# One root chain at each layer norm, a last norm shared with TensorE, and a third conditioning buffer for the tenth weight slot

## The chip, the cores and the metric

The kernel runs on one core of a Trainium2 chip. The metric is the device time of one execution in microseconds (us), lower is better. Before the change three executions gave 2537.12, 2537.58 and 2540.77 us, so the median is 2537.58 us.

## What is computed

Two post-norm layers over 256 tokens of width 2048, all in float32. A conditioning vector `c` gives a shift, a scale and a gate for each sub-layer.

```python
cond = jax.nn.silu(c)
for l in range(DEPTH):                                   # DEPTH = 2
    ada = (cond @ w_ada[l] + b_ada[l])[:, None, :]       # 2048 x 12288 matrix, one row of input
    sh_m, sc_m, g_m, sh_f, sc_f, g_f = jnp.split(ada, N_ADA, axis=-1)
    h = x * (1.0 + sc_m) + sh_m
    y = hybrid_mixer(h, ..., w_in[l], w_out[l], ...)     # h @ w_in (6672 columns), three head groups, @ w_out
    x = layer_norm(DEEPNORM_ALPHA * x + (1.0 + g_m) * y, ln_g[l, 0], ln_b[l, 0])
    h = x * (1.0 + sc_f) + sh_f
    y = jnp.square(jax.nn.relu(h @ w1[l])) @ w2[l]       # width 8192 between
    x = layer_norm(DEEPNORM_ALPHA * x + (1.0 + g_f) * y, ln_g[l, 1], ln_b[l, 1])
```

`layer_norm` is `(x - mean) * rsqrt(var + 1e-5) * g + b` over the 2048 columns.

## The kernel before

**Units and passes.** The tokens are two rows of 128 partitions (r = 0 and 1). Every large matrix product is cut into units: a block of 128 rows of weights by 1024 columns (512 KB). A pass is 16 units that add into four PSUM banks; there are 25 passes in a layer, 0 to 6 for `w_in`, 7 and 8 for `w_out`, 9 to 24 for the MLP in four groups, 800 units in all. To keep float32 accuracy each operand is split into a high part and a rest, and each product is three matrix products. A unit goes this way: SyncE (SP) issues its load into one of ten slots `RAW` (L477); ScalarE copies it to the high part `WH`, one of six slots (`hi_split`, L643); VectorE subtracts to get the rest `WL`, written over `RAW` (`lo_split`, L1024); TensorE multiplies (L1554 for most, L1563 for products that come out transposed, L1522 for the first pass of a sub-layer). Splits run four units ahead of TensorE (`AHEAD`). The load of a unit waits until the unit ten before it is done (`unit_done`).

**Conditioning.** `cond @ w_ada` runs beside the passes on VectorE. A block of 128 rows by 1024 columns of `w_ada` lands in one of two buffers `ADR` (L468), and one VectorE instruction multiplies it by a scalar per partition and adds it to `ACC` (`ada_mul`, L922 and L925). After 16 blocks TensorE sums `ACC` over the partitions (L1456, or L1463 for a gate). A written-out plan, `ADA_PLAN`, says beside which units the 16 blocks of each piece are added, and by which unit the sum is due. In layer 0 it puts nearly one block beside each of the first 50 units, and 16 blocks beside units 93 to 106. SP issues the load of block `a` behind the weight load that is `ADA_LAG` (6) units ahead of its place, and only when block `a - 2` has been added. SP issues in order, so a block that waits holds the weight loads behind it.

**The layer norm between sub-layers.** Of the last four units of passes 8 and 24 TensorE does one PSUM bank at a time (`last_units`, L1536), so that VectorE can begin a quarter (one row r, 512 columns) while TensorE does the next. `quarter` (L1068 to L1077) multiplies the bank by the gate, adds it to X, and takes batch statistics; after the second quarter of a row it aggregates them and prepares the variance. ScalarE takes the square root (L687), `newton` (L1044 to L1048) inverts it and improves it by one Newton step, `rstd` also makes `NMR = -mean * rstd` (L1082), and `norm` (L1087) writes the normed X. Gain and bias of the norm are folded into the next sub-layer's scale and shift. TensorE then transposes X (L1489), ScalarE applies scale and shift (`h_tiles`, L663 and L666), and the next pass starts (L1522). There are three such boundaries. All engines run program order as written; nothing is reordered.

**The last norm** (`last_layer_norm`) needs gain and bias in full: per row r and 512 columns, `centre` (L1121) is `(x - mean) * g` and `finish` (L1127) is `* rstd + b`. SP stores each of the eight pieces when it is finished (L511).

Of the kernel before, what the change touches and what calls it, by code (L numbers as in the profile page):

```python
# [17 lines left out]
P = 128  # L18
# [7 lines left out]
RAW_SLOTS, W_SLOTS = 10, 6  # L26
PRO_SLOTS = 16
AHEAD = 4
ADA_LAG = 6
# [70 lines left out]
def hybrid_trunk(nc, x, c, positions, lb_logits, w_in, w_out, w_ada, b_ada, ln_g, ln_b, hg_norm_w,  # L100
                 m_conv_w, m_conv_b, m_dt_bias, m_a_log, m_d, m_norm_w, w1, w2, consts, out):
    with ExitStack() as ctx:
# [12 lines left out]
        X = sb("X", [P, 2, D])  # L115
        HTh = sb("HTh", [P, KT, SEQ], F32R)
# [10 lines left out]
        ADR = sb("ADR", [P, 2, UW])  # L127
# [29 lines left out]
        NMR = sb("NMR", [P, 2])  # L157
        RV = sb("RV", [P, 8])
# [104 lines left out]
        ada_in = [Signal(f"ada_in{i}", 16 * 96) for i in range(2)]  # L263
# [7 lines left out]
        xT = Signal("xT", 16)  # L271
        hT_hi = Signal("hT_hi", 32)
# [6 lines left out]
        rs_in = Signal("rs_in", 7)  # L279
        rs_act = Signal("rs_act", 7)  # L280
# [134 lines left out]

        def ada_arrived(a):

            return ada_in[a % 2].sem, 16 * ((a - 64) // 2 + 1)
# [43 lines left out]
        def _(sp):  # L462
            def ada_load(a):
                q, k = divmod(a, 16)
                if a >= 64 + 2:
                    sp.wait_ge(ada_mac.sem, ada_added(a - 2))
                row, col = ADA_SEQ[q] // 12 * D + k * P, ADA_SEQ[q] % 12 * UW
                sp.dma_start(ADR[:, a % 2, :], w_ada_r[row:row + P, col:col + UW]).then_inc(ada_in[a % 2].sem, 16)  # L468

# [46 lines left out]
        def _(pool):  # L516
            link = Order(pool, order["pool"])
            pool.memset(RV[:, :], 1.0)
# [82 lines left out]
        def _(act):  # L601
# [52 lines left out]
            def h_tiles(layer, s, b):  # L654

                if b == 0:
                    act.wait_ge(cols_set.sem, cols_set.at(layer, s + 1))
                act.wait_ge(xT.sem, xT.at(layer, 8 * s + b + 1))
                for j in range(2):
                    kt = 2 * b + j  # L660
                    cols = work(s * FF0, b % 4)[:, j * SEQ:(j + 1) * SEQ]
# [22 lines left out]
            def ln_sqrt(layer, s, r):  # L684

                act.wait_ge(rs_in.sem, rs_in.at(layer, 4 + 2 * s + r))
                act.activation(RA[:, r:r + 1], RV[:, r:r + 1], ACT.Sqrt).then_inc(rs_act.sem, 1)  # L687

# [13 lines left out]
            def layer_norm(layer, s, n):  # L702

                ln_sqrt(layer, s, 0)
                for m in range(n - 2, n + 1):
                    next_split(layer, m)
                ln_sqrt(layer, s, 1)
# [203 lines left out]
        def _(dve):  # L911
# [3 lines left out]
            def ada_mul(a):  # L915

                q, k = divmod(a, 16)
                w = ADR[:, a % 2, :]
# [141 lines left out]
            def quarter(layer, s, i, p, k, passes):  # L1060
# [13 lines left out]
                if h == 1:  # L1074
                    link(ins)
                    link(dve.bn_aggr(MV[:, r, :], BN[:, r, :, :].rearrange("p a b -> p (a b)")))
                    ts(RV[:, r:r + 1], MV[:, r, 1:2], LN_EPS, None, ALU.add).then_inc(rs_in.sem, 1)  # L1077

            def rstd(layer, s, r):

                link(newton(layer, 4 + 2 * s + r, slice(r, r + 1)))
                link(stt(NMR[:, r:r + 1], MV[:, r, 0:1], -1.0, RR[:, r:r + 1], ALU.mult, ALU.mult))  # L1082
# [13 lines left out]
            def layer_norm(layer, s, p, k, passes, gate, n):  # L1096
# [18 lines left out]
            def last_layer_norm(layer, p, k, passes, gate):  # L1115

                done = {"mul": 0}

                def centre(r, ch):
                    xc, cols = X[:, r, ch * 512:(ch + 1) * 512], slice(ch * 512, (ch + 1) * 512)  # L1120
                    stt(xc, xc, MV[:, r, 0:1], LNG[:, cols], ALU.subtract, ALU.mult).then_inc(ln_mul.sem, 1)  # L1121
                    done["mul"] += 1

                def finish(r, ch, mul):
                    xc, cols = X[:, r, ch * 512:(ch + 1) * 512], slice(ch * 512, (ch + 1) * 512)
                    dve.wait_ge(ln_mul.sem, mul)
                    stt(xc, xc, RR[:, r:r + 1], LNB[:, cols], ALU.mult, ALU.add).then_inc(x_out.sem, 1)  # L1127
# [3 lines left out]
                dve.wait_ge(ln_gb_in.sem, ln_gb_in.at(layer, 64))  # L1131
                quarter(layer, 1, 0, p, k, passes)
                quarter(layer, 1, 1, p, k, passes)
                centre(0, 0)
                rstd(layer, 1, 0)
                centre(0, 1)
                quarter(layer, 1, 2, p, k, passes)
                finish(0, 0, 1)
                centre(0, 2)
                finish(0, 1, 2)  # L1140
                centre(0, 3)
                quarter(layer, 1, 3, p, k, passes)
                finish(0, 2, 3)
                finish(0, 3, 4)
                centre(1, 0)
                rstd(layer, 1, 1)
                centre(1, 1)
                finish(1, 0, 5)
                centre(1, 2)
                finish(1, 1, 6)  # L1150
                centre(1, 3)
                finish(1, 2, 7)
                finish(1, 3, 8)
# [295 lines left out]
        def _(pe):  # L1449
# [31 lines left out]
            def x_transpose(layer, s, b):  # L1481
# [3 lines left out]
                for r in range(2):  # L1485
                    pe.wait_ge(x_ready.sem, x_ready.at(layer, 6 * s + (r + 1 if b == 0 else 4 if b < 4 else 6)) - 6)
                    for j in range(2):
                        kt = 2 * b + j
                        ins = tr(work(s * FF0, b % 4)[:, j * SEQ + r * P:j * SEQ + (r + 1) * P],  # L1489
                                 X[:, r, kt * P:(kt + 1) * P], ident)  # L1490
                ins.then_inc(xT.sem, 1)
# [339 lines left out]


# [19 lines left out]
```

## Time and profile before

| what | value |
|---|---|
| median of three executions | 2537.58 us |
| the profiled execution | 2538.42 us |
| its span, first to last instruction | 2536.6 us |
| TensorE busy with matrix products | 2418.4 us, 95% of the span |
| VectorE busy | 1893.9 us, 75% |
| ScalarE busy | 1163.9 us, 46% |
| mean granted TensorE clock | 0.99 |
| HBM traffic | 249 GB/s over the span |

How to read it: TensorE is nearly always busy, so time can only be won where it waits or where it runs at the lower clock. In the timelines an instruction has its start, its duration and its shape, and in square brackets the idle time of its engine before it with what ended that. The durations overlap: an instruction of VectorE begins before the one ahead has quite ended, so the step from start to start is what counts.

### The profile page before, as it was taken

The page shows a single profiled execution, that of the slowest core. Times are in us where ns is not written, and L with a number is a line of the kernel's source. Part 1 is how long each engine was busy: PE and PEld are TensorE (multiplying, and loading weights), DVE is VectorE, ACT ScalarE, POOL GpSimd, SP SyncE. Part 2 cuts the span into 40 slices and gives each one's busy share as a digit, 9 for nine tenths or more (in the row PEclk, how much of TensorE's full clock was granted, in tenths as well). Part 3 has the DMA queues.
Part 4 walks back from the last instruction along what each step waited for, and adds up shares of the span by engine and source line. Part 5 has one row for each costly group of instructions (what it writes and reads, how often), then busy time and mean ns, then how long its engine had stood idle before and what let it go on. Part 6 is the DMA issues. An engine that isn't in the chain of part 4 may idle for free.

```text
span 2536.6 us, 36597 instructions
## 1 busy us (share of the span) xinstructions
PE 2418.4 (95%) x14933; PEld 2181.6 (86%) x14933; DVE 1893.9 (75%) x2099; ACT 1163.9 (46%) x1507; POOL 174.7 (7%) x119
## 2 busy tenths in 40 slices
PE   2599999999999999999999999999999999999997
PEld 2599987888989989989979998888898998998986
DVE  7889897878977787878777568868797555555556
ACT  0364475545533534434436446655544353443442
POOL 0002100010011011011010020001001101101001
PEclk9999999999999999999999999999999999999999
DMA  9998577887898898898865535778688656656653
GB/s 389 374 335 287 162 249 243 294 290 258 286 323 320 277 331 301 305 315 295 292 233 158 167 110 178 228 256 300 249 290 291 187 186 192 184 189 192 183 190 109
DMA packets 176396, 634.02 MB, mean 250 GB/s; under 512 B 20236, under 2 KB 20964, under 8 KB 174948
## 3 DMA queue, kind: packets, MB, share of 16 engines
q1 hardware_dynamic: 171648, 614.80, 71.7%
q0 software_dynamic: 3008, 16.32, 1.7%
q8 instruction: 118, 1.93, 0.3%
q10 hardware_dynamic: 1572, 0.56, 0.1%
q14 instruction: 50, 0.41, 0.1%
HBM read 629.50 MB, written 2.10 MB: 249 GB/s over the span
## 4 chain that ended last, share of the span: by engine, by line
PE 85%; DVE 7%; DMA 4%; issue 1%; ACT 1%; SPq 0%; DVEq 0%; ACTq 0%
PE PB L1554 42%; PE PB L1563 29%; PE PB L1522 8%; DMA ADR<-in_w_ada 2%; DMA RAW<-in_w_ada 2%; PE PB L1536 1%; DVE ACC L925 1%; DVE WL L1024 1%; DVE ACC L1015 1%; PE PB L1597 1%; PE PB L1456 1%; DVE CV L1197 1%; PE PB L1463 1%; PE PB L1489 1%; SPq L483 0%
## 5 line engine op out<-in xcount | busy, mean ns | idle before, releaser
L1024 DVE TENSOR_TENSOR WL<-RAW,WH 128x1024 fp32r<-128x1024 f32 (+1 forms) x800 | 994.2, 1250 | 481.4 <-ACT WH L643 480.6
L643 ACT ACTIVATE WH<-RAW 128x1024 fp32r<-128x1024 f32 (+1 forms) x800 | 832.3, 1044 | 1117.0 <-PE PB L1554 537.9
L1563 PE MATMUL PB<-HTh,WH 128*128 128x256 f32 x2176 | 620.9, 285 | 0.0
L1563 PE MATMUL PB<-HTh,WL 128*128 128x256 f32 x2176 | 616.9, 284 | 0.0
L1563 PE MATMUL PB<-HTl,WH 128*128 128x256 f32 x2176 | 616.8, 283 | 0.0
L925 DVE SCALAR_TENSOR_TENSOR ACC<-ADR,CT,ACC 128x1024 f32<-128x1024 f32 x300 | 393.0, 1310 | 59.8 <-DMA ADR<-in_w_ada 57.8
L1563 PEld LDWEIGHTS PB<-HTl,WH 128*128 128x128 f32 x2176 | 418.7, 192 | 0.8 <-issue 0.5
L1563 PEld LDWEIGHTS PB<-HTh,WH 128*128 128x128 f32 x2176 | 418.6, 192 | 0.8 <-issue 0.5
L1563 PEld LDWEIGHTS PB<-HTh,WL 128*128 128x128 f32 x2176 | 418.6, 192 | 0.0
L1554 PE MATMUL PB<-WH,T2h 128*128 128x512 f32 x1208 | 374.4, 391 | 0.0
L1554 PE MATMUL PB<-WL,T2h 128*128 128x512 f32 x1208 | 372.1, 389 | 0.0
L1554 PE MATMUL PB<-WH,T2l 128*128 128x512 f32 x1208 | 371.9, 389 | 0.0
L1554 PEld LDWEIGHTS PB<-WL,T2h 128*128 128x128 f32 x1208 | 226.7, 188 | 47.4
L1554 PEld LDWEIGHTS PB<-WH,T2l 128*128 128x128 f32 x1208 | 226.7, 188 | 47.3
L1554 PEld LDWEIGHTS PB<-WH,T2h 128*128 128x128 f32 x1208 | 225.8, 188 | 47.7 <-issue 1.9
L536 POOL TENSOR_TENSOR X<-X,Y 128x512 f32<-128x512 f32 x64 | 112.5, 1788 | 1356.2 <-DVE Y L1176 1356.2
L1554 PE MATMUL PB<-WH,HTh 128*128 128x512 f32 x512 | 163.9, 401 | 0.6 <-issue 0.6
L1554 PE MATMUL PB<-WL,HTh 128*128 128x512 f32 x512 | 158.8, 391 | 0.0
L1554 PE MATMUL PB<-WH,HTl 128*128 128x512 f32 x512 | 158.2, 390 | 0.0
L1554 PEld LDWEIGHTS PB<-WH,HTl 128*128 128x128 f32 x512 | 96.4, 188 | 20.9
L1554 PEld LDWEIGHTS PB<-WL,HTh 128*128 128x128 f32 x512 | 96.4, 188 | 20.8
L1554 PEld LDWEIGHTS PB<-WH,HTh 128*128 128x128 f32 x512 | 92.7, 189 | 19.1 <-issue 1.5
(288 smaller groups left out, 2124.3 us busy)
## 6 DMA issues: line engine op xcount, KB each, us to landing
RAW<-in_w SPq DMA_DIRECT2D x512, 512.0 KB, 4.6
ADR<-in_w_ada SPq DMA_DIRECT2D x320, 512.0 KB, 5.3
RAW<-in_w_in SPq DMA_DIRECT2D x192, 512.0 KB, 4.2
RAW<-in_w_ada SPq DMA_DIRECT2D x64, 512.0 KB, 15.8
RAW<-in_w_out SPq DMA_DIRECT2D x64, 512.0 KB, 5.9
RAW<-in_w_in SPq DMA_DIRECT2D x32, 264.0 KB, 2.8
GB<-in_b_ada POOLq DMA_DIRECT2D x8, 512.0 KB, 7.6
LNG<-in_ln_g POOLq DMA_DIRECT2D x4, 1024.0 KB, 7.6
```

The source lines that it names most:

```text
L536: pool.tensor_tensor(xc, xc, Y4[:, b, :], ALU.add).then_inc(x_add.sem, 1)
L643: act.activation(WH[:, wh_slot(layer, n), 0:w], RAW[:, k, 0:w], ACT.Copy).then_inc(hi_done.sem, 1)
L925: ins = stt(ACC[:, :], w, CT[:, k:k + 1], ACC[:, :], ALU.mult, ALU.add)
L1015: ins = stt(acc[:, :], block_, CT[:, k:k + 1], acc[:, :], ALU.mult, ALU.add)
L1024: tt(WL[:, k, 0:w], RAW[:, k, 0:w], WH[:, wh_slot(layer, n), 0:w].bitcast(F32), ALU.subtract).then_inc(lo_done.sem, 1)
L1197: ins = stt(dst[:, j, sh:SEQ], src[:, j, 0:SEQ - sh], cCW[:, tap, t:t + 1], dst[:, j, sh:SEQ], ALU.mult, ALU.add)
L1456: ins = mm(bank_ap[:, i:i + 1], ACC[:, i * P:(i + 1) * P], ones, start=True, stop=True)
L1463: ins = mm(work(p, 2 + h)[:, :], ones_all, ACC[:, h * 512:(h + 1) * 512], start=True, stop=True)
L1489: ins = tr(work(s * FF0, b % 4)[:, j * SEQ + r * P:j * SEQ + (r + 1) * P], X[:, r, kt * P:(kt + 1) * P], ident)
L1522: ins = mm(dst, w[:, slot[w is WL], j * P:(j + 1) * P], a[:, kt, :], start=first and i == 0 and j % 2 == 0, stop=last and i == 2, skip_gro ...
L1554: ins = mm(bank(p, 2 * r + h)[:, :], a[:, kt, rows], w[:, slot[w is WL], h * 512:(h + 1) * 512], start=first and i == 0, stop=last and i == 2)
L1563: ins = mm(dst, w[:, slot[w is WL], cols], a[:, kt, :], start=first and i == 0 and j % 2 == 0, stop=last and i == 2, skip_group_check=True)
```

## The change

Three edits. In the diff below the four lines after the boundary's are the bodies of `scaled`, `rest`, `finish` and `finish_low`, in this order.

1. **One root chain.** At the three boundaries VectorE does all four quarters in a run. Then one square root and one Newton chain serve both rows (operands 128x2 and not 128x1). The chain has four instructions and not six, since the epsilon is added in the first fused one, and `norm` subtracts the mean and multiplies, so that `NMR` isn't needed there. The square root reads the variance itself and adds epsilon as its bias. TensorE transposes both rows together and signals after the first tile (`xT_first`); the second tile goes to another PSUM bank (`x_bank`).
2. **The last norm.** X and the gain are multiplied first (`scaled`), four pieces ahead of the first quarter. Row 0 becomes `x*g*rstd + b` (`rest`) and then `+ g*NMR` (`finish`). For row 1 TensorE builds `b + NMR*g` in PSUM by two matrix products per piece, one with the identity and one with the diagonal matrix `DIAG`, and VectorE needs one instruction per piece (`finish_low`).
3. **Buffers.** `RAW_SLOTS` goes from 10 to 9, the conditioning buffers `ADR` from 2 to 3, and `ADA_LAG` from 6 to 5. The load of block `a` now waits for block `a - 3`.

```diff
-RAW_SLOTS, W_SLOTS = 10, 6
+RAW_SLOTS, W_SLOTS, ADR_SLOTS = 9, 6, 3
-ADA_LAG = 6
+ADA_LAG = 5
...
+        def x_bank(layer, s, kt):
+            return work(s * FF0, 3 if kt == 1 and (layer or s) else kt // 2 % 4)
...
-                if a >= 64 + 2:
-                    sp.wait_ge(ada_mac.sem, ada_added(a - 2))
+                if a >= 64 + ADR_SLOTS:
+                    sp.wait_ge(ada_mac.sem, ada_added(a - ADR_SLOTS))
...
+            def newton(count, var, eps, rr, ra):
+                dve.wait_ge(rs_act.sem, count)
+                link(dve.reciprocal(rr, ra))
+                link(stt(ra, var, eps, rr, ALU.add, ALU.mult))
+                link(stt(ra, ra, -0.5, rr, ALU.mult, ALU.mult))
+                return stt(rr, ra, 1.5, rr, ALU.add, ALU.mult)
...
-                ts(xc, xc, RR[:, r:r + 1], NMR[:, r:r + 1], ALU.mult, ALU.add).then_inc(x_ready.sem, 1)
+                ts(xc, xc, MV[:, r, 0:1], RR[:, r:r + 1], ALU.subtract, ALU.mult).then_inc(x_ready.sem, 1)
...
-                for i in range(3):
-                    quarter(layer, s, i, p, k, passes)
-                rstd(layer, s, 0)
-                norm(0, 0, 256)
-                quarter(layer, s, 3, p, k, passes)
-                rstd(layer, s, 1)
-                norm(1, 0, 256)
+                for i in range(4):
+                    aggr = quarter(layer, s, i, p, k, passes)
+                aggr.then_inc(rs_in.sem, 1)
+                rstd(rs_act.at(layer, 4 + s), 0, 2)
+                for r in range(2):
+                    norm(r, 0, 256)
...
+                    tt(xc, xc, LNG[:, ch * 512:(ch + 1) * 512], ALU.mult).then_inc(ln_u.sem, 1)
+                    stt(xc, xc, RR[:, 0:1], LNB[:, cols], ALU.mult, ALU.add).then_inc(ln_mul.sem, 1)
+                    stt(xc, LNG[:, cols], NMR[:, 0:1], xc, ALU.mult, ALU.add).then_inc(x_out.sem, 1)
+                    stt(xc, xc, RR[:, 1:2], work(p, ch)[:, :], ALU.mult, ALU.add).then_inc(x_out.sem, 1)
...
+            for ch in range(4):
+                mm(work(FF0 + 3, ch)[:, :], ident, LNB[:, ch * 512:(ch + 1) * 512], start=True, stop=False)
+            pe.wait_ge(ln_diag.sem, 1)
+            for ch in range(4):
+                mm(work(FF0 + 3, ch)[:, :], DIAG[:, :], LNG[:, ch * 512:(ch + 1) * 512], start=False, stop=True
+                   ).then_inc(ln_w.sem, 1)
```

VectorE at a boundary, before, from the third quarter's statistics on (Y is the gated product, MV mean and variance, RR the inverse root, RA scratch):

```order
L1073 BN_STATS BN<-X 128x6 [waits x_add]
L1044 RECIPROCAL RR<-RA 128x1 [waits rs_act]
L1045 TENSOR_TENSOR RA<-RR 128x1 [waits dve_order]
L1046 TENSOR_TENSOR RA<-RA,RV 128x1 [waits dve_order]
L1047 TENSOR_SCALAR RA<-RA 128x1 [waits dve_order]
L1048 TENSOR_TENSOR RR<-RR,RA 128x1 [waits dve_order]
L1082 SCALAR_TENSOR_TENSOR NMR<-MV,RR 128x1 [waits dve_order]
L1087 TENSOR_SCALAR X<-X,RR,NMR 128x256 [waits dve_order]
L1068 TENSOR_TENSOR Y_143<-PB,GB 128x512 [waits unit_done]
```

VectorE at the same place now, from the same statistics on:

```order
L1094 BN_STATS BN<-X 128x6 [waits x_add]
L1089 TENSOR_TENSOR Y_145<-PB,GB 128x512 [waits unit_done]
L1092 TENSOR_TENSOR X<-X,Y_145 128x512 [waits gated]
L1094 BN_STATS BN<-X 128x6 [waits x_add]
L1097 BN_AGGR MV<-BN 128x2 [waits dve_order]
L1066 RECIPROCAL RR<-RA 128x2 [waits rs_act]
L1067 SCALAR_TENSOR_TENSOR RA<-MV,RR 128x2 [waits dve_order]
L1068 SCALAR_TENSOR_TENSOR RA<-RA,RR 128x2 [waits dve_order]
L1069 SCALAR_TENSOR_TENSOR RR<-RA,RR 128x2 [waits dve_order]
L1106 TENSOR_SCALAR X<-X,MV,RR 128x256 [waits dve_order]
L1106 TENSOR_SCALAR X<-X,MV,RR 128x256
```

The chain and the norm that stood ahead of the last quarter are gone from there, and the one chain behind it is shorter.

VectorE at the end of the program, before, from the last quarter on (LNG and LNB are gain and bias):

```order
L1068 TENSOR_TENSOR Y_143<-PB,GB 128x512 [waits unit_done]
L1071 TENSOR_TENSOR X<-X,Y_143 128x512 [waits gated]
L1073 BN_STATS BN<-X 128x6 [waits x_add]
L1076 BN_AGGR MV<-BN 128x2 [waits dve_order]
L1077 TENSOR_SCALAR RV<-MV 128x1 [waits dve_order]
L1127 SCALAR_TENSOR_TENSOR X<-X,RR,LNB 128x512 [waits ln_mul] x2
L1121 SCALAR_TENSOR_TENSOR X<-X,MV,LNG 128x512
L1044 RECIPROCAL RR<-RA 128x1 [waits rs_act]
...
L1082 SCALAR_TENSOR_TENSOR NMR<-MV,RR 128x1 [waits dve_order]
L1121 SCALAR_TENSOR_TENSOR X<-X,MV,LNG 128x512 [waits dve_order]
L1127 SCALAR_TENSOR_TENSOR X<-X,RR,LNB 128x512 [waits ln_mul]
```

Now, from the same quarter's aggregate to the end:

```order
L1097 BN_AGGR MV<-BN 128x2 [waits dve_order]
L1137 TENSOR_TENSOR X<-X,LNG 128x512
L1066 RECIPROCAL RR<-RA 128x1 [waits rs_act]
...
L1141 SCALAR_TENSOR_TENSOR NMR<-MV,RR 128x1 [waits dve_order]
L1178 TENSOR_SCALAR DIAG<-K,NMR 128x128 [waits dve_order]
L1151 SCALAR_TENSOR_TENSOR X<-LNG,NMR,X 128x512 [waits ln_mul] x2
L1146 SCALAR_TENSOR_TENSOR X<-X,RR,LNB 128x512 x2
L1151 SCALAR_TENSOR_TENSOR X<-LNG,NMR,X 128x512 [waits ln_mul] x2
L1157 SCALAR_TENSOR_TENSOR X<-X,RR,PB 128x512 [waits ln_w,ln_u]
L1157 SCALAR_TENSOR_TENSOR X<-X,RR,PB 128x512 [waits ln_w] x3
```

Behind the last quarter stood ten instructions of 512 columns (two of row 0, eight of row 1); now there are eleven, four of them reading PSUM.

SP at the start of the passes of layer 0, before:

```order
L477 DMA RAW_54<-in_w_in 128x1024 [waits ada_mac] x7
L468 DMA ADR_57<-in_w_ada 128x1024
L477 DMA RAW_54<-in_w_in 128x1024 [waits ada_mac]
L468 DMA ADR_57<-in_w_ada 128x1024
L477 DMA RAW_54<-in_w_in 128x1024 [waits ada_mac]
L468 DMA ADR_57<-in_w_ada 128x1024 [waits ada_mac]
```

And now:

```order
L492 DMA RAW_55<-in_w_in 128x1024 [waits ada_mac] x6
L482 DMA ADR_58<-in_w_ada 128x1024
L492 DMA RAW_55<-in_w_in 128x1024 [waits ada_mac]
L482 DMA ADR_58<-in_w_ada 128x1024
L492 DMA RAW_55<-in_w_in 128x1024 [waits ada_mac]
L482 DMA ADR_58<-in_w_ada 128x1024
```

Three conditioning blocks are issued with no wait where two were, and each stands one weight load earlier in the queue.

## Rows read from the trace of the kernel before

**Rows 1.** The page: its span, and the busy time of TensorE (PE) and VectorE (DVE).

```profile
span 2536.6 us, 36597 instructions
PE 2418.4 (95%) x14933; PEld 2181.6 (86%) x14933; DVE 1893.9 (75%) x2099; ACT 1163.9 (46%) x1507; POOL 174.7 (7%) x119
```

**Rows 2.** Waits of TensorE, whole program: total us, times, longest.

```profile
PE PB L1489 <- DVE X L1087: 14.9, 6, 3.9
```

**Rows 3.** Timeline of VectorE at the second boundary: start us, duration us, instruction.

```profile
1324.64 0.14 DVE L1044 RECIPROCAL RR<-RA 128x1 f32<-128x1 f32 x1
...
1325.79 0.41 DVE L1087 TENSOR_SCALAR X<-X,RR,NMR 128x256 f32<-128x256 f32 x1
1326.11 0.68 DVE L1068 TENSOR_TENSOR Y<-PB,GB 128x512 f32<-128x512 f32 x1
...
1328.28 0.26 DVE L1076 BATCH_NORM_AGGREGATE MV<-BN 128x2 f32<-128x24 f32 x1
1328.58 0.15 DVE L1077 TENSOR_SCALAR RV<-MV 128x1 f32<-128x1 f32 x1
1329.00 0.16 DVE L1044 RECIPROCAL RR<-RA 128x1 f32<-128x1 f32 x1 [0.27 <-ACT RA L687]
...
1330.17 1.59 DVE L1087 TENSOR_SCALAR X<-X,RR,NMR 128x256 f32<-128x256 f32 x3
```

**Rows 4.** Timeline of ScalarE at the same boundary.

```profile
1323.32 2.96 ACT L643 ACTIVATE WH<-RAW 128x1024 fp32r<-128x1024 f32 x3 [0.59 <-PE PB L1536]
```

**Rows 5.** Timeline of TensorE at the same boundary.

```profile
1324.87 0.39 PE L1536 MATMUL PB<-WH,T2l 128*128 128x512 f32 x1
...
1330.63 0.69 PE L1489 MATMUL PB<-K,X 128*128 128x128 f32 x2 [3.94 <-DVE X L1087]
1332.13 2.05 PE L1522 MATMUL PB<-HTh,WH 128*128 128x256 f32 x8 [0.81 <-ACT HTh L663]
...
1337.36 1.20 PE L1522 MATMUL PB<-HTh,WH 128*128 128x256 f32 x8
```

**Rows 6.** Busy times in two stretches: length, PE, PEld, DVE, ACT, POOL, clock, DMA.

```profile
1329.70:1336.50 6.80, 5.06 (x22) 4.69 (x23) 5.49 (x11) 2.88 (x5) 0.00 (x0) 0.50 0.12 49
...
459.30:462.70 3.40, 3.40 (x18) 3.40 (x17) 3.40 (x4) 0.00 (x0) 0.00 (x0) 0.50 0.64 201
```

**Rows 7.** Timeline of VectorE at the end of the program.

```profile
2507.08 1.21 DVE L1024 TENSOR_TENSOR WL<-RAW,WH 128x1024 fp32r<-128x1024 f32 x1
...
2513.45 0.69 DVE L1068 TENSOR_TENSOR Y<-PB,GB 128x512 f32<-128x512 f32 x1 [1.85 <-PE PB L1536]
...
2523.17 0.68 DVE L1068 TENSOR_TENSOR Y<-PB,GB 128x512 f32<-128x512 f32 x1
...
2532.16 1.41 DVE L1127 SCALAR_TENSOR_TENSOR X<-X,RR,LNB 128x512 f32<-128x512 f32 x2
```

**Rows 8.** The chain that ended last: start us, us, a gate's two sums.

```profile
1681.75 1.72 PE PB L1463 x4
```

**Rows 9.** Waits of TensorE in the passes of layer 0's mixer, 106 to 576 us.

```profile
PE PB L1757 <- DVE SR L1365: 1.9, 1, 1.9
...
PE PB L1554 <- issue: 0.6, 1, 0.6
```

**Rows 10.** Waits of VectorE for conditioning blocks, 425 to 458 us.

```profile
DVE ACC L925 <- DMA ADR<-in_w_ada: 8.0, 9, 2.0
```

**Rows 11.** Waits of SP's queue in the same stretch.

```profile
SPq L468 <- DVE ACC L925: 27.4, 11, 3.7
```

**Rows 12.** Busy times in two stretches, columns as in rows 6; the last is GB/s.

```profile
0.00:63.00 63.00, 15.23 (x69) 14.70 (x69) 49.24 (x57) 4.31 (x9) 1.38 (x10) 1.00 1.00 389
425.00:458.00 33.00, 31.00 (x149) 25.46 (x147) 26.20 (x30) 15.90 (x19) 0.60 (x1) 1.00 0.92 322
```

**Rows 13.** Waits of all engines: ScalarE for the weights of the output projection.

```profile
ACT WH L643 <- DMA RAW<-in_w_out: 22.6, 12, 5.0
```

**Rows 14.** The chain that ended last: one unit of TensorE.

```profile
343.26 2.75 PE PB L1554 x12
```

More of the change, by code:

```diff
@@ L115, in hybrid_trunk @@
         X = sb("X", [P, 2, D])
+        DIAG = sb("DIAG", [P, P], at=place["at"])
         HTh = sb("HTh", [P, KT, SEQ], F32R)
@@ L262, in hybrid_trunk @@
         set_free = Signal("set_free", 7)
-        ada_in = [Signal(f"ada_in{i}", 16 * 96) for i in range(2)]
+        ada_in = [Signal(f"ada_in{i}") for i in range(ADR_SLOTS)]
         ada_mac = Signal("ada_mac", 192, 64 + 2)
@@ L682, in rsqrt, with ln_sqrt @@
                 act.activation(RA[:, 0:cols], RV[:, 0:cols], ACT.Sqrt).then_inc(rs_act.sem, 1)
[L684 to L687 removed]
+            def ln_sqrt(count, r0, r1):
+                act.wait_ge(rs_in.sem, count)
+                act.activation(RA[:, r0:r1], MV[:, r0:r1, 1], ACT.Sqrt, bias=EPS[:, 0:1]).then_inc(rs_act.sem, 1)
             def scale_ln(layer, s):
@@ L1115, in last_layer_norm, with scaled, row_rstd, rest @@
             def last_layer_norm(layer, p, k, passes, gate):
[L1117 to L1127, printed above, removed]
+                def scaled(r, ch):
+                    xc = X[:, r, ch * 512:(ch + 1) * 512]
+                    tt(xc, xc, LNG[:, ch * 512:(ch + 1) * 512], ALU.mult).then_inc(ln_u.sem, 1)
+                def row_rstd(r):
+                    rstd(rs_act.at(layer, 5 + r), r, r + 1)
+                    link(stt(NMR[:, r:r + 1], MV[:, r, 0:1], -1.0, RR[:, r:r + 1], ALU.mult, ALU.mult))
+                def rest(ch):
+                    xc, cols = X[:, 0, ch * 512:(ch + 1) * 512], slice(ch * 512, (ch + 1) * 512)
+                    stt(xc, xc, RR[:, 0:1], LNB[:, cols], ALU.mult, ALU.add).then_inc(ln_mul.sem, 1)
+                def finish(ch):
+                    xc, cols = X[:, 0, ch * 512:(ch + 1) * 512], slice(ch * 512, (ch + 1) * 512)
+                    dve.wait_ge(ln_mul.sem, ch + 1)
+                    stt(xc, LNG[:, cols], NMR[:, 0:1], xc, ALU.mult, ALU.add).then_inc(x_out.sem, 1)
+                def finish_low(ch):
+                    xc = X[:, 1, ch * 512:(ch + 1) * 512]
+                    dve.wait_ge(ln_w.sem, ch + 1)
+                    stt(xc, xc, RR[:, 1:2], work(p, ch)[:, :], ALU.mult, ALU.add).then_inc(x_out.sem, 1)
                 dve.wait_ge(ada_cols.sem, cols_at(layer, gate))
@@ L1131, in last_layer_norm @@
                 dve.wait_ge(ln_gb_in.sem, ln_gb_in.at(layer, 64))
+                for r in range(2):
+                    for ch in range(2):
+                        scaled(r, ch)
                 quarter(layer, 1, 0, p, k, passes)
[L1133 to L1136, printed above, removed]
+                scaled(0, 2)
+                quarter(layer, 1, 1, p, k, passes).then_inc(rs_in.sem, 1)
+                scaled(0, 3)
+                row_rstd(0)
                 quarter(layer, 1, 2, p, k, passes)
[L1138 to L1153, printed above, removed]
+                scaled(1, 2)
+                dve.wait_ge(ln_u.sem, 7)
+                rest(0)
+                rest(1)
+                quarter(layer, 1, 3, p, k, passes).then_inc(rs_in.sem, 1)
+                scaled(1, 3)
+                row_rstd(1)
+                ts(DIAG[:, :], ident, NMR[:, 1:2], None, ALU.mult).then_inc(ln_diag.sem, 1)
+                finish(0)
+                finish(1)
+                rest(2)
+                rest(3)
+                finish(2)
+                finish(3)
+                dve.wait_ge(ln_u.sem, 8)
+                for ch in range(4):
+                    finish_low(ch)
             def residual(layer, s, ch, part):
@@ L1484, in x_transpose @@
                     pe.wait_ge(hT_tx.sem, hT_tx.at(layer, 16 * s + 2 * (b - 4) + 2))
-                for r in range(2):
-                    pe.wait_ge(x_ready.sem, x_ready.at(layer, 6 * s + (r + 1 if b == 0 else 4 if b < 4 else 6)) - 6)
-                    for j in range(2):
+                if b == 3 and (layer or s):
+                    pe.wait_ge(hT_tx.sem, hT_tx.at(layer, 16 * s + 2))
+                pe.wait_ge(x_ready.sem, x_ready.at(layer, 6 * s + (2 if b == 0 else 4 if b < 4 else 6)) - 6)
+                for j in range(2):
+                    for r in range(2):
                         kt = 2 * b + j
-                        ins = tr(work(s * FF0, b % 4)[:, j * SEQ + r * P:j * SEQ + (r + 1) * P],
+                        ins = tr(x_bank(layer, s, kt)[:, j * SEQ + r * P:j * SEQ + (r + 1) * P],
                                  X[:, r, kt * P:(kt + 1) * P], ident)
+                    if b == 0 and j == 0:
+                        ins.then_inc(xT_first.sem, 1)
                 ins.then_inc(xT.sem, 1)
```

55 lines of the change are left out of this document (32 added, 23 removed).

## The prediction

> **What bounds the kernel now.** I read the page first, then TensorE's waits, then the timelines where it waits. In the page look at TensorE: busy 2418.4 of 2536.6 us [rows 1]. VectorE, busy 1893.9 us, is second. So only three kinds of time can be won: TensorE's waits, the stretch behind its last product, and work done at its lower clock. Among the waits look for the boundary: transposes waited 14.9 us in six waits, two at each of three boundaries, the longest 3.9 us [rows 2]. Then the mixer of layer 0: 1.9 us for VectorE's masked scores and 0.6 us at the start of a pass [rows 9]. Last look at VectorE just before that 1.9 us wait: it had itself waited 8.0 us for conditioning blocks within 33 us [rows 10].
>
> **Part 1, the three boundaries.** The second stands for all; the others repeat its steps. Four things change in the chain from TensorE's last product to its next pass.
> a) Before the last quarter (1326.11) VectorE did the first chain and a norm, from 1324.64 [rows 3]. TensorE's last product began at 1324.87 and lasted 0.39, so its bank was ready at 1325.26 [rows 5], and with a tenth for the signal the quarter can begin at 1325.35. VectorE is free by then (1324.64). Won: 0.76 us.
> b) The variance step between aggregate and root, 1328.28 to 1328.58, is gone: 0.30 us.
> c) From the inverse (1329.00) to the norm (1330.17) six small instructions took 1.17 us, 0.195 each; four remain: 0.39 us. That they are two elements wide I cost at nothing.
> d) The norm of row 0 now stands ahead of row 1's: its step was 1325.79 to 1326.11, lost 0.32 us.
> Sum 1.13 us. The root stays one step of 0.42 us; ScalarE's three weight splits that now stand ahead of it end at 1326.28 [rows 4], before the root is wanted at about 1327.8. From the second norm to the first product (1330.17 to 1332.13) nothing changes: two transposes stand ahead of the signal, as before. The added wait of the fourth pair of transposes for ScalarE's second tile has three units between and costs nothing; what is queued behind it on TensorE is the unit after.
>
> This start falls in a stretch at half clock: 0.50 from 1329.70 to 1336.50 [rows 6], the 1.2 GHz level, and eight products took 2.05 us there against 1.20 us at full clock [rows 5]. If the full clock comes back at the same moment as before, what starts 1.13 us earlier does so at half speed and is worth 0.57 us. I take 1.0 us a boundary, near the upper bound, since the idle time that lowered it gets shorter too. Three: 3.0 us, bounds 1.7 and 3.4.
>
> **Part 2, the last norm.** VectorE is free at 2507.08 + 1.13 = 2508.2 [rows 7]. Four `scaled` at 0.6 each end at 2510.6, the first quarter (three steps of 0.7) at 2512.7, a fifth `scaled` at 2513.3. The second quarter's bank was ready at 2513.45 [rows 7], so all of that is hidden. Each bank costs 18 products of 0.227 us, 4.08 us: the third is ready at 2517.5, the fourth at 2521.6. Quarter 1, aggregate, a `scaled` and five small instructions end at 2517.4; quarter 2, a `scaled` and two `rest` end at 2521.65. So the last quarter begins at 2521.65 and not at 2523.17: 1.5 us won. Behind its start stood 10.4 us (to 2532.16 + 1.41 = 2533.57). Now: quarter and aggregate 2.4, `scaled` 0.6, five small ones 1.0, the diagonal 0.2, six of 0.66 make 4.0, four `finish_low` at 0.7 make 2.8: 11.0 us, half a microsecond more. End at 2532.6, 1.0 us won. The stores behind it (3.0 us to the span's end) stay.
>
> TensorE's part: two products of this kind took 1.72 us [rows 8], 0.86 each. Four with the bias end at 2525.0, hidden; four with the diagonal begin at about 2525.9 and end at 2529.4, the first `finish_low` wants one at 2529.8. So hidden too. At half clock the last would be ready at 2532.8 and cost 0.9 us; and a PSUM operand in the fused form, which no row shows, may step by 0.66 or by 0.8. Bounds 0 and 1.3 us.
>
> **Part 3, the buffers.** Look at SP's queue from 425 to 458 us: for 27.4 of 33 us it stood waiting for VectorE to have added block a - 2 [rows 11], while VectorE waited 8.0 us for blocks, at most 2.0 at once [rows 10]. The pair ran as a loop of two buffers and a transfer. In these 33 us 11 blocks were issued, one in 3.0 us, so with the wait on a - 3 each can be issued up to 3.0 us earlier, more than the longest wait. If half of the 8.0 us goes, VectorE is at the scores 4 us earlier, and TensorE's 1.9 us wait and the 0.6 us one are gone [rows 9]. I take 2.3 of 2.5 us, bounds 0 and 2.5. Behind the 1.9 us wait the clock was at half for 3.4 us, 459.30 to 462.70 [rows 6]; without the wait that may be gone, worth 1.7 us, or fall elsewhere. I take 0.9 us, bounds -1.7 and 1.7.
>
> The price is the weight slot: a load may start one unit, 2.75 us [rows 14], later. Its cover is the split four units ahead (11 us). ScalarE waited 22.6 us for the output projection's weights, 12 times [rows 13], and no TensorE wait followed, so I take nothing. Where the queue was held by conditioning blocks, weight loads behind them even start earlier. The shorter Newton chain inside the mixers, an epsilon tile and the lag (its gate is again the unit four before) I cost at nothing: no wait of TensorE stands on them.
>
> Against this part speaks the share of the DMA engines: 0.92 in that stretch, at 322 GB/s [rows 12]. If it is full, a third buffer only moves the queue. For it speaks that the same engines moved 389 GB/s in the first 63 us [rows 12], so a fifth more was possible. The Trainium skill (DMA: Bandwidth & Descriptors, "Where 436 GB/s comes from") states that transfers from HBM are bound near 358 GB/s per core, and measures 425 GB/s for 16 MB. By its lower figure the stretch would be within a tenth of its limit; the 389 GB/s here do not agree with that figure.
>
> **Sum.** 3.0 + 1.0 + 2.3 + 0.9 = 7.2 us. The profiled execution took 2538.42 us, 1.8 more than its span; less 7.2 it is 2531.2 us. It stood 0.84 above the median, and by the median it would be 2530.4. I say 2531.0 us. About 0.2%, 5.1 us, is what a measurement here can tell from no change; faster begins at 2532.5.
>
> **Rivals.**
> B, the transfers are full and the third buffer brings nothing: parts 1 and 2 alone, 4.0 us, 2533.6 to 2534.4 us. For it: the share of 0.92. Against it: 389 GB/s [rows 12] and the 27.4 us on a buffer [rows 11]. Chance 0.25.
> C, the half clock takes part 1 back and part 3 brings nothing: 1.7 + 0.8 = 2.5 us, 2535.5 us. Chance 0.09.
> D, slower: nine weight slots are too few where transfers are near full. The place is the output projection, with its 12 waits [rows 13], and such stretches in the first passes. It decides once the weights come later than the four units of lead; then each place costs one unit, 2.75 us. Four such places, 11.0 us, less the 4.0 of parts 1 and 2, give about 2545 us. Against it: TensorE shows no wait for a split at all. Chance 0.05.
> E, more than the sum: a half-clock stretch behind a boundary is half as long (3.4 of 6.8 us, worth 1.7), and the one at 459 goes in full with another like it: 11.5 us, 2526.5 us. Chance 0.11.
> The forecast has 0.50, with its own range 2529 to 2533.5.
>
> **How the numbers follow.** Faster: 0.44 of the forecast's 0.50, 0.11 of E and 0.05 of B, 0.60. Slower: 0.05. Same: the rest, 0.35. The range is 2526 to 2536.5: it holds the forecast, B, C and most of E.
>
> **What would show it.** At each boundary the last quarter begins within 0.2 us of TensorE's last product, and 6.87 - 1.13 = 5.7 us lie from there to the first product of the next pass (1325.26 to 1332.13 before). The last quarter of the program starts at 2521.65 less all that was won before it, and the store's tail stays 3.0 us. Between the blocks VectorE's waits fall well below 8.0 us, SP's queue waits for units and not for VectorE, and the 1.9 us wait is missing. Wrong would be: the waits for blocks stay and the engines' share is 1.0 (B); or TensorE shows waits for `WL` (D).

## The result and the profile after

The changed kernel takes 2523.32 us (median of four executions, 2522.47 to 2524.64) against 2538.23 us for the one before on the same chip (four executions, 2537.12 to 2540.77). The ratio is 0.9942, 95% interval 0.9930 to 0.9954: 14.9 us faster. The forecast was 2531.0 us with a range down to 2526: the direction was right, the forecast gain of 7.2 us is half of the measured one, and the time lies below the range. Medians leave out three executions at a clearly lower clock (3474, 4662 and 2713 us, at a mean granted clock of 0.66, 0.90 and 0.85).

The page of the changed kernel, the answer to [rows 1]:

```profile
span 2522.2 us, 36597 instructions
PE 2417.9 (96%) x14949; PEld 2179.6 (86%) x14949; DVE 1889.7 (75%) x2064; ACT 1164.2 (46%) x1504; POOL 173.7 (7%) x120
```

TensorE's busy time is nearly the same, though 7.3 us of new products at the end of the program are in it and some work at the lower clock has gone from it. The span is 14.4 us shorter.

**Where the time went.** I lined up the two traces by the end of each unit, the last product that raises `unit_done`, and subtracted. Of the 14.4 us of span:

| stretch | before, us | after, us | difference |
|---|---|---|---|
| start to the end of unit 31, layer 0 | 201.07 | 201.55 | +0.48 |
| units 32 to 111 (passes 2 to 6) | 286.39 | 277.62 | -8.77 |
| units 112 to 143 | 91.37 | 90.59 | -0.78 |
| three boundaries with the unit behind each | 35.60 | 32.51 | -3.09 |
| mixer of layer 1 | 451.46 | 450.20 | -1.26 |
| both MLPs (735.00 and 720.66) | 1455.66 | 1455.68 | 0.0 |
| last product to the end | 15.03 | 14.06 | -0.97 |

Waits of TensorE in the mixer of layer 0, 106 to 576 us, the answer to [rows 9]:

```profile
PE PB L1525 <- DVE X L1106: 4.5, 1, 4.5
PE PB L1649 <- DVE SM L1250: 2.0, 1, 2.0
PE PB L1767 <- DVE MW L1384: 1.5, 1, 1.5
PE PB L1560 <- DVE HTl L1052: 1.2, 1, 1.2
PE PB L1767 <- DVE XS L1392: 0.9, 1, 0.9
PE PB L1560 <- ACT HTh L682: 0.6, 1, 0.6
```

The 1.9 us for the masked scores is gone and so is the 0.6 us. The first row is the boundary, which now begins before 576 us.

VectorE's waits around the scores, 418 to 452 us, that answer to [rows 10] have no row for blocks any more. SP's queue in the same stretch, the answer to [rows 11], and the busy times of 418 to 452 us, the answer to [rows 12]; then the low stretch at the second boundary, the answer to [rows 6]:

```profile
SPq L482 <- DVE ACC L947: 17.7, 10, 3.2
SPq L492 <- PE PB L1592: 6.2, 3, 2.7
```

```profile
418.00:452.00 34.00, 34.00 (x170) 28.81 (x169) 32.18 (x37) 15.90 (x19) 0.59 (x1) 1.00 0.99 366
1319.20:1326.00 6.80, 6.27 (x28) 5.90 (x29) 5.60 (x9) 2.88 (x5) 0.00 (x0) 0.50 0.15 61
```

TensorE fills the stretch and VectorE nearly does (32.2 of 34 us), and the transfers rose from 322 to 366 GB/s at a share of 0.99. So there was room. Whether any is left the share can't tell: at a share of 1.00 the same engines moved 389 GB/s [rows 12].

The second boundary on VectorE, the answer to [rows 3]:

```profile
1314.96 0.69 DVE L1089 TENSOR_TENSOR Y<-PB,GB 128x512 f32<-128x512 f32 x1 [0.57 <-PE PB L1574]
...
1317.15 0.27 DVE L1097 BATCH_NORM_AGGREGATE MV<-BN 128x2 f32<-128x24 f32 x1
1317.77 0.17 DVE L1066 RECIPROCAL RR<-RA 128x2 f32<-128x2 f32 x1 [0.36 <-ACT RA L706]
...
1318.56 1.92 DVE L1106 TENSOR_SCALAR X<-X,MV,RR 128x256 f32<-128x256 f32 x4
```

On ScalarE the root before, then the split copies, now ahead of the root [rows 4], and the root now:

```profile
1328.77 0.20 ACT L687 ACTIVATE RA<-RV 128x1 f32<-128x1 f32 x1 [2.48 <-DVE RV L1077]
```

```profile
1312.98 2.95 ACT L659 ACTIVATE WH<-RAW 128x1024 fp32r<-128x1024 f32 x3 [7.78 <-PE PB L1574]
1317.44 0.29 ACT L706 ACTIVATE RA<-MV,EPS 128x2 f32<-128x2 f32 x1 [1.51 <-DVE MV L1097]
```

And on TensorE, the answer to [rows 5]:

```profile
1314.54 0.39 PE L1574 MATMUL PB<-WH,T2l 128*128 128x512 f32 x1
1319.35 1.11 PE L1525 MATMUL PB<-K,X 128*128 128x128 f32 x4 [4.42 <-DVE X L1106]
1320.85 2.05 PE L1560 MATMUL PB<-HTh,WH 128*128 128x256 f32 x8 [0.38 <-ACT HTh L682]
```

From TensorE's last product (1314.93) the quarter starts after 0.03 us (0.85 before: 0.82 won). From aggregate to inverse it takes 0.62 us, 0.72 before: 0.10 won and not 0.30. The variance step is gone, but the root now takes 0.29 us where it took 0.20, and it starts 0.29 us behind the start of the step that releases it (1317.15 to 1317.44) where that was 0.19 us (1328.58 to 1328.77). Inverse to norm takes 0.79 us (0.38 won), the second norm costs 0.33. Last product to first product is 5.92 us against 6.87: 0.95 won at this boundary, 1.13 forecast.

The end of the program on VectorE, the answer to [rows 7], and TensorE's part of it, for [rows 8]:

```profile
2508.27 0.69 DVE L1089 TENSOR_TENSOR Y<-PB,GB 128x512 f32<-128x512 f32 x1
...
2516.31 2.72 DVE L1157 SCALAR_TENSOR_TENSOR X<-X,RR,PB 128x512 f32<-128x512 f32 x4
```

```profile
2507.98 3.59 PE L1873 MATMUL PB<-LNB,K 128*128 128x512 f32 x8
2512.47 3.70 PE L1876 MATMUL PB<-LNG,DIAG 128*128 128x512 f32 x8 [0.90 <-DVE DIAG L1178]
```

The last quarter starts at 2508.27; the forecast's 2521.65 less the 13.43 us won until then is 2508.22. TensorE's diagonal products end at 2516.17, just before the first `finish_low`.

### The profile page after: what moved, and what is told of

Read it like the earlier page. It is cut to its first block, busy times and chain, and to the rows that moved or that the text cites. A ratio compares the mean times of both kernels' runs of the same rounds, so it can differ in the third digit from the quotient of the medians.

```text
span 2522.2 us, 36597 instructions
## 1 busy us (share of the span) xinstructions
PE 2417.9 (96%) x14949; PEld 2179.6 (86%) x14949; DVE 1889.7 (75%) x2064; ACT 1164.2 (46%) x1504; POOL 173.7 (7%) x120
## 4 chain that ended last, share of the span: by engine, by line
PE 91%; DVE 5%; DMA 2%; issue 1%; ACT 1%; SPq 0%; DVEq 0%; ACTq 0%
PE PB L1592 46%; PE PB L1601 30%; PE PB L1560 8%; DMA RAW<-in_w_ada 2%; PE PB L1574 2%; DVE ACC L1037 1%; PE PB L1490 1%; DVE WL L1046 1%; PE PB L1635 1%; PE PB L1497 1%; PE PB L1525 1%; DVE CV L1231 0%; DVE ACC L947 0%; PE PB L1767 0%; DVE MS L1248 0%
## 5 line engine op out<-in xcount | busy, mean ns | idle before, releaser
L1592 PEld LDWEIGHTS PB<-WH,T2l 128*128 128x128 f32 x1208 | 226.8, 188 | 47.3
```

The costliest lines, as they stand in the source:

```text
L1592: ins = mm(bank(p, 2 * r + h)[:, :], a[:, kt, rows], w[:, slot[w is WL], h * 512:(h + 1) * 512], start=first and i == 0, stop=last and i == 2)
```

## The experiments

All against the kernel before on the same chip in the same session; its median moved between 2537.5 and 2541.2 us from session to session. Since sessions differ, the mechanism is read from the traces, by the same stretches:

| kernel | weight slots, buffers, lag | median us (n) | lowest to highest | units 32 to 111 | three boundaries | mixer of layer 1 |
|---|---|---|---|---|---|---|
| before, first trace | 10, 2, 6 | 2538.23 (4) | 2537.1 to 2540.8 | 286.39 | 35.60 | 451.46 |
| before, again | 10, 2, 6 | 2541.12 (1) | | 286.43 | 35.53 | 452.44 |
| new norms only | 10, 2, 6 | 2534.03 (6) | 2528.8 to 2535.7 | 289.85 | 32.02 | 451.20 |
| lag 5, two buffers | 10, 2, 5 | 2540.95 (10) | 2534.0 to 2546.5 | 290.13 | 30.75 | 451.19 |
| slot away | 9, 2, 5 | 2540.78 (10) | 2531.4 to 2546.1 | 293.33 | 31.87 | 451.24 |
| third unused | 9, 3, 5 | 2539.87 (9) | 2535.8 to 2544.1 | 293.94 | 33.26 | 450.56 |
| buffers only | 9, 3, 5 | 2527.39 (4) | 2526.3 to 2529.1 | 277.81 | 36.10 | 450.54 |
| changed, first trace | 9, 3, 5 | 2523.32 (4) | 2522.5 to 2524.6 | 277.62 | 32.51 | 450.20 |
| changed, again | 9, 3, 5 | 2522.55 (1) | | 277.64 | 31.85 | 451.16 |
| lag 6, three buffers | 9, 3, 6 | 2523.38 (4) | 2522.3 to 2524.9 | 277.61 | 31.79 | 451.15 |
| four buffers | 8, 4, 4 | 2524.30 (5) | 2522.9 to 2525.1 | 277.63 | 33.01 | 450.18 |

The stretches of "new norms only" are from a later execution (2539.58 us), which is not in its median. Every stretch is from one execution.

**Buffers only.** The kernel before with the third edit.

```diff
-RAW_SLOTS, W_SLOTS = 10, 6
+RAW_SLOTS, W_SLOTS, ADR_SLOTS = 9, 6, 3
-ADA_LAG = 6
+ADA_LAG = 5
-                if a >= 64 + 2:
-                    sp.wait_ge(ada_mac.sem, ada_added(a - 2))
+                if a >= 64 + ADR_SLOTS:
+                    sp.wait_ge(ada_mac.sem, ada_added(a - ADR_SLOTS))
```

> The kernel before with only the three buffer edits (nine weight slots, three conditioning buffers, lag 5). Theory (the buffers are worth far more than I forecast, since VectorE then comes in time everywhere in layer 0's mixer): TensorE's start of the MLP of layer 0 comes 8.6 to 9.6 us earlier, and the whole is 8.5 to 11 us shorter than before, about 2527 to 2529.5 us. Rival (the forecast's size was right, the rest is where the low clock happened to fall): about 3 us from the buffers, 2534 to 2536 us, with low-clock stretches at other places.

2527.39 us, ratio 0.9946 (0.9929 to 0.9962): by the medians 13.8 us less (interval 9.7 to 18 us), more than the 11 us expected; the kernel before had its highest median, 2541.22 us, beside this run. By the trace it is 10.0 us of span, 8.58 of them in units 32 to 111. The theory held by the trace; the rival that the forecast's size was right fell. VectorE's waits for blocks in the mixer of layer 0, 34.3 us before (35 times), here:

```profile
DVE ACC L925 <- DMA ADR<-in_w_ada: 7.2, 7, 2.5
```

**New norms only.** The changed kernel with the old numbers.

```diff
-RAW_SLOTS, W_SLOTS, ADR_SLOTS = 9, 6, 3
+RAW_SLOTS, W_SLOTS, ADR_SLOTS = 10, 6, 2
-ADA_LAG = 5
+ADA_LAG = 6
```

> The changed kernel with ten weight slots, two conditioning buffers and lag 6 again, so only the boundaries and the last norm are new. Theory: 3.1 us at the three boundaries and 1.0 us at the end, about 2534 us; TensorE again waits 1.9 us for the masked scores. Rival (earlier starts also moved the work in the mixers off its waits): 2530 us or less with two buffers.

> The norms-only kernel once more for its trace (ten slots, two buffers, lag 6). Theory: boundaries 3.1 us and end 1.0 us shorter than before, the mixer of layer 0 with the same waits as before; what differs there is where the low clock falls, up to 2 us per stretch.

Median of seven executions, six and one later, 2534.32 us, from 2528.8 to 2539.6; ratio of the first six 0.9965 (0.9949 to 0.9981), 4.8 to 13 us. The spread of 11 us is too wide to tell 4.1 from 8. The trace is clear on the boundaries (3.6 us shorter) and the end (0.9 us, 15.03 to 14.1); the scores' wait is back, at 2.5 us, and units 32 to 111 are even 3.5 us longer than before in this execution. The rival, 2530 us or less, is met by two executions and not by the median.

**The slot away, and the lag.** Nine slots, two buffers, lag 5; then ten slots, two buffers, lag 5.

```diff
-RAW_SLOTS, W_SLOTS, ADR_SLOTS = 9, 6, 3
+RAW_SLOTS, W_SLOTS, ADR_SLOTS = 9, 6, 2       # the second kernel: 10, 6, 2
```

> The changed kernel with two conditioning buffers but nine weight slots and lag 5: the price of the slot without its use. Theory: the slot costs nothing, same as with ten slots within 1 us, about 2534 us. Rival (the weight loads are late where transfers are near full, hidden in the change by the gain of the third buffer): 1 to 4 us slower than that, with waits of TensorE in the output projection.

> The changed kernel with ten weight slots and two conditioning buffers, lag 5: against nine slots with the same lag (the run with the slot away, mixer 7 us longer) it tells slot from lag. Theory (it is the tenth slot: a weight load held behind a waiting block has one unit less to land): the mixer of layer 0 is as long as before within 1.5 us and ScalarE's waits for w_in weights fall from 59 us to under 15 us. Rival (the lag: blocks one place earlier in the queue hold more weight loads): the mixer stays 5 us or more longer than before.

2540.78 us (ratio 0.9995, 0.998 to 1.001) and 2540.95 us (1.0011, 0.9999 to 1.0024): the gain of the norms is eaten. My theory of the slot fell in both. The rivals were not met in full either: in the first TensorE has no wait in the output projection (units 112 to 143 take 90.59 us as in the changed kernel), and in the second units 32 to 111 are 3.7 us longer than before, not 5. ScalarE's waits for weights in the mixer of layer 0, without the slot and then with it:

```profile
ACT WH L659 <- DMA RAW<-in_w_in: 59.2, 30, 4.3
```

```profile
ACT WH L659 <- DMA RAW<-in_w_in: 63.7, 32, 4.6
```

With lag 6 and ten slots it is 8.3, 17.0 and 16.9 us (the kernel before twice, the norms-only kernel). So with two buffers the lag raises these waits: a block one place earlier in SP's queue holds the weight loads behind it while it waits for its buffer. That it also costs time is read from the medians alone, 2534.0 us with lag 6 and 2540.95 us with lag 5, from two sessions, with intervals against the kernel before that don't overlap; the one trace of each has units 32 to 111 within 0.3 us (289.85 and 290.13). That the tenth slot is worth something with two buffers, no time shows (0.2 us between the medians).

**Third buffer in memory, not used for the wait.**

```diff
-                if a >= 64 + ADR_SLOTS:
-                    sp.wait_ge(ada_mac.sem, ada_added(a - ADR_SLOTS))
+                if a >= 64 + 2:
+                    sp.wait_ge(ada_mac.sem, ada_added(a - 2))
```

> The changed kernel with three conditioning buffers in memory, but the load of block a still waits for block a - 2. Theory (the wait on the buffer is what the third one removes): the waits of VectorE for blocks come back to 6 to 9 us in the 33 us around the masked scores of layer 0, and the time is that with two buffers, about 2534 us. Rival (order and lag do it): stays near 2523 us.

2539.87 us, ratio 0.9999 (0.9988 to 1.001). The whole gain of the buffers is gone, VectorE waits 8.4 us for blocks in the 33 us around the scores (6 to 9 expected), and 59.2 us of waits for weights are there again. So what gains is the removal of the wait on block a - 2, and nothing else of the edit. I had said about 2534; it is 6 us slower, about what the lag costs with two buffers by the medians above, which I didn't have then.

**Lag 6 with three buffers; four buffers.** One constant in the first; 8, 6, 4 and lag 4 in the second.

> The changed kernel with lag 6 and nine slots, three buffers. Theory: the load of a block is then gated by the unit three before its place and not four, 2.75 us later, so the waits of VectorE for blocks in layer 0's mixer rise from 6 us to 20 us or more, and the kernel is 4 to 8 us slower than the changed one, 2527 to 2531 us. Rival (the wait on block a - 2 alone was the cause, the lag is without weight): within 1.5 us of the changed one.

> One step further the same way: eight weight slots, four conditioning buffers, lag 4, all else as changed. Theory (what gains is that neither SP's queue nor VectorE waits for a buffer): with three buffers 6 us of waits for blocks are left in layer 0's mixer and TensorE has no wait of that kind, so a fourth brings nothing, and one slot fewer costs up to 2 us: 2523 to 2526 us. Rival (slots and buffers are exchanged one for one and more buffers stay better): 2520 us or less.

2523.38 us and 2524.30 us, both within 1 us of the changed kernel. The theory on four buffers held. The theory on the lag fell: VectorE's waits for blocks do rise, to 14.2 us, but TensorE waits no more than before, and units 32 to 111 take 277.61 us. With four buffers there is no wait for a block at all, and ScalarE waits 21.1 us for weights instead; 277.63 us. So three are enough, and what remains there isn't the transfers.

**The same kernels again.**

> The kernel before, unchanged, once more, for its trace: 15 more executions of it lie between 2534.5 and 2543.1 us. Theory (with two buffers each late transfer is passed on to VectorE and TensorE, so executions differ in the stretches where blocks are dense): against the first trace it differs between units 31 and 111 of layer 0 by 1 us or more, and by less than 1 us over the MLP. Rival: the difference lies at the boundaries and in the low clock alone.

> The changed kernel, unchanged, once more, for its trace. Theory: with three buffers the same stretches, units 31 to 111, agree with its first trace within 0.5 us; the boundaries may differ by up to 1.7 us each with the length of the low stretch behind them.

The changed kernel agrees with its first trace within 0.02 us over units 32 to 111. The kernel before takes the same sum (0.04 us apart), where the theory had 1 us or more, so by its own measure the theory fell. It takes it in other steps: counted from unit 31, it is 2.2 us later than the first execution at unit 47 and 0.9 us earlier at unit 95, and its wait for the scores is 3.1 us and not 1.9. It also differs by 2.7 us over an MLP, where a low stretch stands at 945.8 us, which the theory excluded.

**A wait put in.** Work on VectorE ahead of the scores of layer 0.

```diff
                         if at == (6, 6):
+                            for _ in range(20 if layer == 0 else 0):
+                                link(tt(SM[:, :], K[:, 0:P], K[:, 0:P], ALU.mult))
```

> The changed kernel with 20 small instructions (128x128, each waiting for the one before, about 0.32 us a piece, 6.4 us in all) put on VectorE ahead of the masked scores of layer 0, where it now is 4 us early. They write a scratch tile that nobody reads. Theory (a wait of TensorE of 2 us costs itself and a stretch at the low clock behind it): TensorE waits about 2.4 us there, a stretch of 3.4 us at half clock follows at about 455 us, and the kernel is about 4 us slower, 2527 to 2528 us. Rival (the low clock has nothing to do with that wait): 2.4 us slower, no stretch there.

2527.76 us (2524.7 to 2529.3), 4.4 us slower. TensorE waits, and the clock falls right behind it:

```profile
453.04 0.49 PE L1797 MATMUL PB<-RVv,SR 128*128 128x128 f32 x2 [2.99 <-DVE SR L1401]
```

```profile
453.80:457.20 3.40, 3.40 (x18) 3.40 (x17) 3.40 (x4) 0.00 (x0) 0.00 (x0) 0.50 0.28 54
```

Units 32 to 111 take 282.55 us, 4.93 more, for a wait of 2.99: it costs itself, 0.2 us of overlap, and 1.7 us of slow clock. The rival of 2.4 us and no low stretch fell. This is the price that the forecast had at half.

**Waits taken out by another plan.** The blocks of piece 9 spread wider.

```diff
-ADA_PLAN = [[(6, 0, 18), (7, 19, 34), (8, 35, 50), (9, 75, 92), (4, 93, 106), (5, 107, 134),
+ADA_PLAN = [[(6, 0, 18), (7, 19, 34), (8, 35, 50), (9, 56, 92), (4, 93, 106), (5, 107, 134),
```

> The changed kernel with the conditioning blocks of one piece spread over units 56 to 92 and not 75 to 92, since VectorE is busy without a gap from 360 to 380 us, where TensorE then waits 1.5 and 0.9 us for it. Theory: these two waits go, and the low stretch at 380 us with them: 3 to 4 us faster than the changed kernel, 2519 to 2521 us. Rival (the blocks now fall among the mixer's masks in passes 3 and 4 and make these late, or the low clock moves): 2522 us or more.

2525.0 us (2522.3 to 2527.0), not faster, as the rival had it. The two waits of pass 5 went with the low stretch at 380 us. The masks of pass 3, for which TensorE waited 2.0 us, now take a wait of 6.0 us with 6.8 us at the lower clock behind it, from 302.5 us, where it was 3.4:

```profile
PE PB L1649 <- DVE SM L1250: 6.0, 1, 6.0
```

So the spread may not begin before unit 64. With `(9, 64, 92)`:

> The changed kernel with the blocks of that piece spread over units 64 to 92: clear of the masks of pass 3 (units 48 to 63), where the spread over 56 to 92 made TensorE wait 6.0 us, and still off the dense run of pass 5. Theory (a wait of TensorE for VectorE costs itself and up to 1.7 us of low clock, wherever it is): the waits of 1.5 and 0.9 us and the low stretch at 380 us go, nothing comes for them before unit 64, 3 to 4 us faster than the changed kernel's 2523.3, about 2519.5 us. Rival (VectorE's work in passes 4 and 5 has no room and the wait only moves again): 2522 us or more, with a wait of 2 us or more between units 64 and 95.

2519.61 us (2518.85 to 2521.07), ratio to the kernel before 0.9919 (0.9901 to 0.9937). The changed kernel's first trace and this one in the stretch of pass 5:

```profile
360.00:380.00 20.00, 18.53 (x85) 14.23 (x84) 20.00 (x20) 12.07 (x20) 0.00 (x0) 1.00 0.88 295
```

```profile
360.00:380.00 20.00, 20.00 (x96) 15.70 (x95) 19.90 (x19) 12.32 (x21) 0.00 (x0) 1.00 0.83 277
```

The 1.5 us wait is gone, and so is the low stretch at 380.5 us, with units 32 to 111 at 274.49 us, 3.13 less; the 0.9 us wait stays, against the theory. This is the fastest version: the change and one number of the plan.

## Why the prediction was wrong

**Right: part 1.** Forecast 3.0 us with bounds 1.7 and 3.4; the first trace shows 3.09. Steps a), c) and d) came out as 0.82, 0.38 and 0.33 against 0.76, 0.39 and 0.32; only b) was 0.10 and not 0.30. Over all traces the three boundaries take 35.5 to 36.1 us with the old norm (three traces) and 30.8 to 33.3 us with the new (eight in the table): the low stretch behind a boundary is 3.4 or 6.8 us long (10.2 once), and the same kernel shows both. The means of the two groups are 3.6 us apart, above my upper bound of 3.4. That the first pair comes out at 3.0 is in part luck: of its 3.09 us the second boundary, from which I took the steps, gives only 0.59, and the other two 1.25 each.

**Right: part 2.** 1.0 us forecast, 0.97 measured, and the last quarter starts within 0.05 us of the place computed. From its start to the end of VectorE's work it takes 10.76 us, forecast 11.0; the instruction with a PSUM operand steps by about 0.68 us (2.72 us for four), not by 0.8.

**Wrong: part 3, the size of "I take 2.3 of 2.5 us" and "I take 0.9 us".** Together 3.2 us; measured 9.55 us from unit 31 to the boundary of layer 0 (8.77 and 0.78). Three errors. First, I counted two waits of TensorE (1.9 and 0.6 us). The first trace before has more in these passes, most of them on VectorE behind a late block, and all gone in the changed one: 0.59 us ahead of L1583 (which the profile calls "issue"), 0.47 and 0.34 us ahead of a sum (L1456), 0.54 us ahead of a gate's sums (L1463), and 0.28 us of the masks' wait (2.31 to 2.03). With 1.86 and 0.59 that is 4.7 us in seven places. Second, a wait costs about 0.15 us more in the step from product to product than its row says, since durations overlap (2.99 us of wait, 3.2 us of step): 1.1 us for seven. Third, two low stretches hung on them, at 213.5 and at 459.3 us, 1.7 us each; I had one, at half its price. The wait put in shows that price: 4.93 us for 2.99. 4.7 + 1.1 + 3.4 is 9.2 of the 9.55 us. So the step that failed is the count of TensorE's waits and the price of the clock behind them, not the sum's other terms. The waits before that I left out, in the stretch of [rows 9] (of the 2.3 us 2.0 stay), and the low stretch that I didn't count:

```profile
PE PB L1611 <- DVE SM L1216: 2.3, 1, 2.3
PE PB L1456 <- DVE ACC L925: 0.8, 2, 0.5
PE PB L1583 <- issue: 0.6, 1, 0.6
PE PB L1463 <- DVE ACC L925: 0.5, 1, 0.5
```

```profile
213.50:216.90 3.40, 3.40 (x18) 3.40 (x18) 2.64 (x4) 0.26 (x1) 1.52 (x1) 0.50 0.75 284
```

**Outside the sum: the mixer of layer 1,** 1.26 us less. The wait of 2.3 us for the masks is in every trace, old kernel or new, with a low stretch behind it in nine of fourteen traces: units 448 to 463 take 47.3 us with it and 45.8 us without. The first trace of the changed kernel is one without. It is chance, not gain; its second trace has it.

**The mechanism** was right: the loop of two buffers and a transfer, [rows 10] and [rows 11]. With the third the queue waits 17.7 us and not 27.4 for VectorE in that stretch. One sign failed in part: I had the queue wait for units and not for VectorE, and it waits 6.2 us for units and still most for VectorE. Rival B fell, since the transfers went from 322 to 366 GB/s. Rival D fell too: TensorE waited for no weights in any kernel with three buffers. Rival E, given 0.11, was the nearest: its second term, the low stretch at 459 with another like it, is what happened. Its time, 2526.5 us, is still 3 us too long. Costing the lag at nothing was right with three buffers and not with two.

**Open.** Why the clock falls behind some waits and not behind others of the same length (nine of fourteen) no run here tells. The traces do show one place where short waits are enough: the 16 products of one column each that sum a piece of conditioning. In the six traces in which a load waits for block a - 2 ("before" to "third unused" in the table), ten such sums had a wait of 0.08 to 0.47 us ahead of them, and a low stretch began within 3.2 us of eight of these; two more low stretches stood behind a sum without a wait. In the eight traces with three or four buffers no sum had a wait and no low stretch stands behind one. The new norms' gain in the median isn't settled with two buffers: in the trace it is 4.1 us, and the interval of the norms-only kernel begins at 4.8. With three buffers the executions lie closer: buffers only 2526.3 to 2529.1 us, changed 2522.5 to 2524.6, medians 4.1 us apart, though in different sessions. Part of the old kernel's spread of 10 us and more (2534.2 to 2545.3 over the sessions) lies in low stretches in the MLP, one of them, at 945.8 us, behind such a sum; the rest was not traced.

## What to carry to other kernels

When a second engine runs at the edge of being late, list every wait of the bounding engine that ends on it, the small ones too, before pricing a buffer. Price each with the slow clock behind it: here a wait of 3.0 us cost 4.9. Where one in-order queue issues two streams, the stream with too few buffers delays the other too, and the place where it stands in the queue then matters; with enough buffers neither lag nor slots could be measured.

## What was not expected of the hardware

- Two buffers and a transfer of 512 KB, with one needed every 3 us, left the transfer engines at a share of 0.92 and 322 GB/s; a third took them to 0.99 and 366 GB/s. The Trainium skill (DMA: Bandwidth & Descriptors, "Where 436 GB/s comes from") puts the bound for transfers from HBM near 358 GB/s per core; the 366 here, over 34 us, is close to it and does not show that it binds, and 389 GB/s over the first 63 us [rows 12] is above it.
- The clock fell to its lower level, 1.2 GHz, behind waits of 1.5 to 3.0 us of TensorE, though not behind each, and stayed there for 3.4 us of full work; behind a wait of 6.0 us it stayed for 6.8 us. At 213.5 us it fell behind two waits of 0.59 and 0.47 us and 16 products of one column.
- Plain float32 products of 512 columns step by 0.45 us, two to a product (3.59 us for eight), against 0.227 us for the rounded kind that the units use.
- With two buffers ten executions of a kernel lie up to 15 us apart (2531.4 to 2546.1 us); in the table's kernels with three or four (and their wait on them) four or five executions lie 2.2 to 2.7 us apart, in the two experiments with a longer wait of TensorE 4.6 and 4.7 us.
